# Prompt attention in one block against two chunks with a middle state, and sample keys and values stacked by matmul against by transfer

## What is computed

```python
D = bcum[..., :, None] - bcum[..., None, :] + li[..., None, :]      # causal
inter = bcum + m[..., None]
m_t = jnp.maximum(inter, jnp.max(D, axis=-1))
w_intra, w_inter = jnp.exp(D - m_t[..., None]), jnp.exp(inter - m_t)
s = jnp.einsum('bhjd,bhsd->bhjs', qc, kc) * w_intra
num = einsum('bhjs,bhsd->bhjd', s, vc) + w_inter[..., None] * einsum('bhvk,bhjk->bhjv', C, qc)
C_new = decay[..., None, None] * C + jnp.einsum('bhs,bhsv,bhsk->bhvk', w_s, vc, kc)
```

## Time and profile before

| | |
|---|---|
| median of 3 runs | 941.18 us (940.92 to 941.48) |
| span of the profiled execution | 940.7 us |
| the four heads | about 75 to 430 us of it |
| TensorE busy (matmul / weight load) | 928.3 / 907.8 us |
| VectorE, ScalarE, GpSimd busy | 772.2, 464.4, 106.7 us |

### The profile page before, as it was taken

One profiled execution on the slowest core, in us unless ns is written; L12 is line 12 of the kernel. 1 busy time (PEld: TensorE's weight loads), 2 busy tenths in 40 slices (PEclk: granted clock), 3 DMA queues, 4 the chain that ended last, 5 costly groups with the idle time before them and its releaser, 6 DMA issues. The chain is left out here.

```text
span 940.7 us, 18449 instructions
## 1 busy us (share of the span) xinstructions
PE 928.3 (99%) x6833; PEld 907.8 (96%) x6833; DVE 772.2 (82%) x1231; ACT 464.4 (49%) x684; POOL 106.7 (11%) x110
## 2 busy tenths in 40 slices
PE   8999999999999999999999999999999999999996
PEld 8999999999999999999999999999999999999995
DVE  6899985988698869876455569999888999889997
ACT  6654452445336324634833345456545555455664
POOL 3011330042006001500231000000000000000001
PEclk9999999999999999999999999999999999999998
DMA  6245216211620352042342222233222223232122
GB/s 219 68 150 198 69 57 224 90 45 56 246 90 23 134 191 90 23 150 87 117 140 68 89 73 84 90 108 106 102 90 91 90 68 113 90 116 109 46 91 100
DMA packets 22460, 98.56 MB, mean 105 GB/s; under 512 B 2929, under 2 KB 5122, under 8 KB 17909
## 3 DMA queue, kind: packets, MB, share of 16 engines
q1 hardware_dynamic: 19576, 77.13, 24.9%
q0 software_dynamic: 1984, 19.72, 5.7%
q10 hardware_dynamic: 832, 0.88, 0.3%
HBM read 85.28 MB, written 12.44 MB: 104 GB/s over the span
## 5 line engine op out<-in xcount | busy, mean ns | idle before, releaser
L1301 PE MATMUL ps<-h_hi,w_hi 128*128 128x288 f32 x896 | 193.7, 298 | 0.0
L1301 PE MATMUL ps<-h_lo,w_hi 128*128 128x288 f32 x896 | 191.7, 295 | 0.0
L1301 PE MATMUL ps<-h_hi,w_lo 128*128 128x288 f32 x896 | 191.4, 295 | 0.0
L793 ACT ACTIVATE w_hi<-raw 128x1024 fp32r<-128x1024 f32 x76 | 80.4, 1058 | 177.4 <-PE ps L1301 174.2
L1301 PEld LDWEIGHTS ps<-h_hi,w_hi 128*128 128x128 f32 x896 | 143.5, 189 | 1.3 <-issue 0.6
L1301 PEld LDWEIGHTS ps<-h_hi,w_lo 128*128 128x128 f32 x896 | 144.3, 189 | 0.0
L1301 PEld LDWEIGHTS ps<-h_lo,w_hi 128*128 128x128 f32 x896 | 144.2, 188 | 0.0
L1692 DVE TENSOR_TENSOR w_lo<-raw,w_hi 128x1024 fp32r<-128x1024 f32 x76 | 94.2, 1240 | 48.9 <-ACT w_hi L793 48.8
L1917 DVE SCALAR_TENSOR_TENSOR conv<-a_p,vec,conv x120 | 97.6, 813 | 0.2
L1569 PE MATMUL ps<-cols_b,late 128*128 128x288 f32 x432 | 62.8, 295 | 0.1
L1569 PE MATMUL ps<-cols_a,main 128*128 128x288 f32 x432 | 62.9, 295 | 0.0
(11 more groups left out here) (362 smaller groups left out, 1857.3 us busy)
## 6 DMA issues: line engine op xcount, KB each, us to landing
raw<-w_head_in SPq DMA_DIRECT2D x40, 512.0 KB, 3.5
raw<-w_fp_in SPq DMA_DIRECT2D x18, 1024.0 KB, 4.9
cs<-st_c_in POOLq DMA_DIRECT2D x4, 2048.0 KB, 9.6
c_s_out<-cs POOLq DMA_DIRECT2D x4, 2048.0 KB, 7.7
raw<-w_fo_in SPq DMA_DIRECT2D x8, 1024.0 KB, 4.9
x<-xT_in SPq DMA_DIRECT2D x16, 288.0 KB, 4.1
raw<-w_cgcv_in SPq DMA_DIRECT2D x8, 512.0 KB, 3.6
raw<-w_ga_in SPq DMA_DIRECT2D x8, 512.0 KB, 3.5
```

Of the source, the lines that this page charges most:

```text
L793: act.activation(w_hi[:, s, :], raw[:, s, :], ACT.Copy).then_inc(hi_ready, 1)
L1301: last = pe.matmul(ps[:, 2 * s + b, 0:HALF], wt[:, w, k * P:k * P + P], src[:, k, b * HALF:b * HALF + HALF], start=(k == 0 and wt is w_hi ...
```

## The change

The prompt's 512 tokens are taken as two chunks of 256. Scores and PV are computed within a chunk only (S widths 256, 128, 256, 128; six pairs of blocks instead of ten). The state after 256 tokens (`CM`, "middle state") is computed after unit 6 from the first two key blocks, copied by ScalarE to `cm32`, and split into `cm_hi` (ScalarE) and `cm_lo` (VectorE). The queries of the second chunk are weighted (`wq`, `qt`) and split (`qt_hi` by ScalarE, `qt_lo` by VectorE), and twelve fp32r products add their reading of the middle state into the PV banks of blocks 2 and 3. CP takes the last two key blocks only, and VectorE adds the decayed middle state to it, reading the bank (before, ScalarE copied). The placement matmuls, `place3` and ScalarE's `stk` copies go; instead ScalarE issues six transfers per head from SBUF to SBUF, and TensorE and GpSimd wait for them. `wvs` is in two tensors now, and `wvn` lies over k alone, so that it no longer waits for the last use of q. A few rows of the setup (decay exponents) are changed accordingly.

```diff
-READER = ["dve"] * 5 + ["act"] * (5 + 1 + 2 + 5 + 2) + ["dve"] * (8 + 1 + 3)
+READER = ["dve"] * 5 + ["act"] * (5 + 1 + 2 + 5) + ["dve"] * (2 + 8 + 1 + 3)
-W_OFF = [0, 512, 896, 1152, 1280]
+S_END = [TP // 2, TP // 2, TP, TP]
+W_OFF = [0, 256, 384, 640, 768]
...
@@ GpSimd, per head
-                    pool.wait_ge(act_read, h * ACT_USES + (START + READER[:K_USE + g].count("act") + 1))
-                    pool.tensor_tensor(wvs[0:3 * GT, g * SG:g * SG + SG, :],
+                    pool.wait_ge(stk_placed[g], h * 48 + 48)
+                    pool.tensor_tensor(wvs[g][0:3 * GT, :, :],
...
@@ ScalarE, per head
-                    for t in range(s + 1, NB):
+                    for t in range(s + 1, S_END[s] // P):
...
+                for t in range(CHUNK):
+                    at = (CHUNK + t) * P
+                    act.activation(wq[:, t * P:t * P + P], negm[...at:at + P...], ACT.Exp, bias=dec[...D_Q + t...])\
+                        .then_inc(w_ready, 1)
                 hi_of(3)
                 for j in range(4, 6):
                     hi_of(j)
                     evac_bias(h, j, halves(qkv[:, 2, :, :], j - 4))
+
+                act.wait_ge(qt_ready, h + 1)
+                act.activation(qt_hi[:, :, :], qt[:, :, :], ACT.Copy).then_inc(pvhi_ready, 1)
...
                 act.activation(inter[0:TS, :], bank(I_USE)[0:TS, 0:HD + SB], ACT.Copy).then_inc(act_read, 1)
+                act.wait_ge(kvsplit_ready, h * 2 + 2)
                 for g in range(2):
-                    use(K_USE + g)
-                    act.activation(stk[0:3 * GT, g, :], bank(K_USE + g)[0:3 * GT, :], ACT.Copy).then_inc(act_read, 1)
+                    for r, src in enumerate(stacked):
+                        act.dma_start(stk[r * GT:r * GT + GT, g, :].rearrange("p (c v) -> p c v", c=2).bitcast(F32),
+                                      src[g * GT:g * GT + GT, :, :].bitcast(F32)).then_inc(stk_placed[g], 16)
+                for k in range(2):
+                    use(CM_USE + k)
+                    act.activation(cm32[:, k, 0:VE], bank(CM_USE + k)[:, 0:VE], ACT.Copy).then_inc(act_read, 1)
 
                 act.wait_ge(dve_read, h * DVE_USES + (START + 5))
                 act.activation(w2_hi[:, :], wts[:, 0:W_OFF[NB]], ACT.Copy).then_inc(pvhi_ready, 1)
                 act.wait_ge(act_read, h * ACT_USES + (START + 5))
                 act.activation(v_hi[:, :, :], kvn[:, 0:NB, HD:2 * HD + 2], ACT.Copy).then_inc(pvhi_ready, 1)
+                act.wait_ge(act_read, h * ACT_USES + (START + 8))
+                act.activation(cm_hi[:, :, :], cm32[:, :, :], ACT.Copy).then_inc(pvhi_ready, 1)
...
-                act.wait_ge(cp_free, h + START)
-                for k in range(2):
-                    use(CP_USE + k)
-                    act.activation(cp[:, k, :], bank(CP_USE + k)[:, 0:VE], ACT.Copy).then_inc(act_read, 1)
@@ TensorE, per head
-                    t0, n, rows_ = (s * P, TP - s * P, P) if s < NB else (TP, TS, TS)
+                    t0, n, rows_ = (s * P, S_END[s] - s * P, P) if s < NB else (TP, TS, TS)
...
-                pe.wait_ge(kvsplit_ready, h * 2 + 2)
-                for g in range(2):            (the eight placement matmuls)
...
+                pe.wait_ge(wv_ready, h * NB + CHUNK)
+                for k in range(2):
+                    use(CM_USE + k)
+                    for s in range(CHUNK):
+                        last = pe.matmul(bank(CM_USE + k)[:, 0:VE], kvn[:, s, k * P:k * P + P], wvn[:, s, :],
+                                         start=(s == 0), stop=(s == CHUNK - 1))
                     last.then_inc(attn_ready, 1)
                 head_unit(7)
...
-                        pe.wait_ge(pvlo_ready, h * 2 + 2)
+                        pe.wait_ge(pvlo_ready, h * N_PV + 3)
+                    if t == CHUNK:
+                        pe.wait_ge(pvlo_ready, h * N_PV + 4)
-                        for s in range(t + 1):
+                        for s in range(t - t % CHUNK, t + 1):
...
+                        for k in range(2 if t >= CHUNK else 0):
+                            at = (t - CHUNK) * P
+                            for q_, c_ in ((qt_hi, cm_hi), (qt_hi, cm_lo), (qt_lo, cm_hi)):
+                                last = pe.matmul(bank(PV_USE + t)[:, 0:VE + 1], q_[:, k, at:at + P], c_[:, k, :],
+                                                 start=False, stop=(k == 1 and q_ is qt_lo))
...
-                    for s in range(NB):
+                    for s in range(CHUNK, NB):                      (CP)
...
+                for g in range(2):
+                    pe.wait_ge(stk_placed[g], h * 48 + 48)
                 pe.wait_ge(wvs_ready, h * 2 + 2)
@@ VectorE, per head
+                dve.wait_ge(w_ready, h * N_W + N_W)
+                dve.wait_ge(gb_used, h * 2 + START)
+                dve.tensor_tensor(qt[:, :, :], qkv[:, 0, :, CHUNK * P:TP], wq[...], ALU.mult).then_inc(qt_ready, 1)
                 lo_of(4)
                 split_lo(h * PER_HEAD + (U_B + 7), 1)
...
                 taps(5)
+                dve.wait_ge(pvhi_ready, h * N_PV + 1)
+                dve.tensor_tensor(qt_lo[:, :, :], qt[:, :, :], qt_hi[:, :, :].bitcast(F32), ALU.subtract)\
+                    .then_inc(pvlo_ready, 1)
...
-                use(I_USE)
                 for s in range(NB):
-                    dve.wait_ge(act_read, h * ACT_USES + (START + s + 1))
-                    dve.tensor_scalar(wvn[:, s, :], kvn[:, s, HD:2 * HD + 1], hcol(I_WS + s), None, ALU.mult)\
+                    dve.tensor_scalar(wvn[:, s, :], kvn[:, s, HD:2 * HD + 1], hcol(I_WV[s]), None, ALU.mult)\
                         .then_inc(wv_ready, 1)
...
+                dve.wait_ge(pvhi_ready, h * N_PV + 4)
+                dve.tensor_tensor(cm_lo[:, :, :], cm32[:, :, :], cm_hi[:, :, :].bitcast(F32), ALU.subtract)\
+                    .then_inc(pvlo_ready, 1)
 
                 lo_of(6)
                 lo_of(7)
...
                 dve.tensor_tensor(small[:, 1, :], small[:, 1, :], small[:, 0, :], ALU.mult).then_inc(hvar_ready, 1)
+                dve.wait_ge(cp_free, h + START)
+                for k in range(2):
+                    use(CP_USE + k)
+                    dve.scalar_tensor_tensor(cp[:, k, :], cm32[:, k, 0:VE], dec[...D_MID...],
+                                             bank(CP_USE + k)[:, 0:VE], ALU.mult, ALU.add).then_inc(dve_read, 1)
                 for b in range(SB):
                     use(CS_USE + b)
```

More of the change, by code:

```diff
@@ L247, in build @@
         warm = sb("warm", 1)
+        tmp_base = place[0]
         tmp = sb("tmp", [2, T])
@@ L319, in build @@
         cp = sb("cp", [2, VE])
+        cm32 = sb("cm32", [2, VE + 1])
+        cm_lo = sb("cm_lo", [2, VE + 1], F32R)
         cs_lo_base = place[0]
@@ L1796, in _ @@
             first = slice(TP, T, SL)
-            steps.on(dve.tensor_tensor(t8[:, :], lf[:, first], m0[:, :], ALU.add))
+            steps.on(dve.tensor_tensor(t8[:, 0:SB], lf[:, first], m0[:, :], ALU.add))
             steps.on(dve.tensor_tensor_scan(ft[0:NH, :], seg[:, :], lf[:, :], 0.0, ALU.mult, ALU.add))
```

141 lines of the change are left out of this document (79 added, 62 removed).

## The result

The changed kernel takes 959.16 us (median of 4 runs, 957.41 to 959.4) against 941.33 (940.92 to 941.66) for the kernel before: a ratio of 1.018, 95% interval 1.0165 to 1.0194. The profiled execution has a span of 957.8, 17.1 more than the profile of before. The forecast was 948.8 with a range of 939 to 956: the direction was right, and what was forecast (+7.6) is less than half of what came (+17.8).

A forecast was written before the change was run, and what follows sets the result against it. TensorE, busy 99%, was taken as the bound; 2.65 us less matmul work per head would be outweighed by waits, mainly for VectorE at the third state update: 941.2 + 4 x 1.9 = 948.8 us, range 939 to 956.

The forecast's parts named there:

- wait in the scores: Fourth score block: TensorE waits for VectorE to read the first block's bank, +0.7 us per head.
- six issues on ScalarE: ScalarE's queue ahead of the weights' high part: six transfer issues at 0.33 to 0.41 each, 2.0 to 2.5 us.
- split of unit 8: VectorE's list: this split begins at 219.45 instead of 218.17, 1.3 us late, or 220.05 with late landing.
- third update: TensorE's third state update can start at 230.3 against 228.53, after VectorE's read frees the bank.
- D: The forecast case for the whole kernel: 944 to 953 us, 58% chance.
- E: Clock falls in the 3 us wait, three k-steps cost twice: +2 to +3 us per head more, 957 to 960; 9%.
- +1.9 per head: Net delay taken for each of four heads, between first-order and late-landing results, nearer the first; +7.6 us in all.
- the walk's first result: First-order walk through one head to the third state update: +1.75 us per head.
- rival F: Transfers slow or each issue at 0.63 us: +3 us per head, 953 to 955; 4%.
- the ledger of matmul work: TensorE per head: scores -1.70, placement -0.95, weights times values 0, state 0; sum -2.65 us.
- rival B: Port free: GpSimd's products out of VectorE's way, third state update 1.0 us earlier, 937.1 us; 15%.
- 0, but moved forward: State matmuls: four ahead of unit 7, four behind; sum unchanged, 1.70 us per head moved forward.

The follow-up runs named there:

- e1: Changed kernel with twelve matmuls of a constant, into columns nobody reads, filling TensorE's wait ahead of the third state update: 952.24 us.
- e13: e10 with ScalarE reading the end state's two banks again, VectorE adding the middle state in SBUF after the state updates: 937.81 us.
- e10: Changed kernel with SyncE issuing the six transfers and ScalarE making the high parts of weights and values before waiting for the middle state: 946.98 us.
- e3: Changed kernel with one of GpSimd's two products per head left out, the states of samples 4 to 7 not computed: 952.59 us.
- e5: Changed kernel with convolution taps moved from ahead of the middle state and from behind the split of unit 8 to behind the state updates: 956.68 us.
- e6: e5 with VectorE's split of unit 7's weights also put behind the products of scores and decay weights: 956.17 us.
- e12: Changed kernel with the taps and splits of e6 and the SyncE issues and ScalarE order of e10, state updates at their old places: 945.68 us.
- e9: Kernel before, with only its placement matmuls and ScalarE's two copies replaced by the six ScalarE-issued transfers: 956.71 us.
- e7: Kernel before, with only one edit: VectorE, not ScalarE, reads the end state's two banks: 943.73 us.
- e4: Changed kernel with the six transfers per head issued by SyncE's queue instead of ScalarE's: 957.52 us.
- e2: Changed kernel with ScalarE reading the end state's banks again, VectorE adding the middle state in SBUF after the eight updates: 944.22 us.

## Why the prediction was right and where it was wrong

By its own steps, in us after the start of the scores (forecast on 193.04, measured on 198.23):

| step | forecast | measured |
|---|---|---|
| wait in the scores | 0.7 | 0.63 |
| scores, without it | 3.1 | 3.35 |
| wait ahead of the middle state, and its start | 0.9, 17.7 | 0.79, 17.72 |
| six issues on ScalarE | 2.0 to 2.5 | 3.84 |
| landing of a transfer | 1.9 | 2.0 |
| first product of GpSimd | 20.5 | 20.54 |
| high part of the weights | 20.3 | 21.62 |
| split of unit 8 | 26.4 to 27.0 | 26.79 |
| from there to the third update | 10.84 | 11.06 |
| third update | 37.3 | 37.85 |
| wait ahead of it | 2.8 | 2.63 |
| clock behind it | stays | halves |

**The step that failed is the choice between D and E: that the clock stays through the wait.** The prediction had the wait of nearly 3 us, named the fall of the clock behind it, priced it at 2 to 3 us per head and its outcome at 957 to 960, and gave it 9%. It happened in all four heads and the time was 959.2. e1 shows it as cause: with the same wait filled, the kernel takes 952.2 and D's own range of 944 to 953 holds. The price was too high; it is 7.0 in all, not 8 to 12. That E's total of 957 to 960 was met all the same is partly luck: the waits cost more than the +7.6 under it (e1: +10.8), and the two errors cancel. The 9% were too few. The one row on the matter, showed half the clock where TensorE works with gaps, and there was no row of a pause of this length inside full work that left the clock alone: the waits of the kernel before lay at its ends. And the range was said to take in the lower part of E, but it ends at 956 and E begins at 957, so it held nothing of E. The Trainium skill, TensorE: Matmul & The Clock Gate, Part 1, has idle stretches throttle the array; here the trace agrees (0.50 of the clock from 237.4 to 240.8, behind 2.63 us of waiting).

**A term mis-sized: +1.9 per head was +2.4** (37.85 against 35.49). Against the walk's first result, +1.75, that is 0.6 us more: 0.4 come ahead of the split of unit 8 and 0.2 in the list behind it. Issues took 0.64 each and not 0.33 to 0.41; the forecast's upper bound, 0.63, was the truth. So rival F's cost of an issue came true, but not its +3 per head: a high part 1.3 us later delays the split by 0.4, because, by the prediction's own walk, the low part would have stood behind the first product anyway. Also the ledger of matmul work is -2.43 per head and not -2.65: scores -1.44 (4.79 to 3.35; I took a record's whole duration difference, but the next matmul starts before a record ends), placement -1.05, products +0.14, states -0.08. It closes: 88.50 - 2.43 + the 1.40 of waits in e13 is 87.47, and e13's heads are 87.4 to 87.6 apart.

**Right for the wrong reason: the bound of the third update.** I took VectorE's list from the split of unit 8 as the only thing that sets it, and rival B (937.1) as what happens when that list starts early. There are two bounds, and both belong to the change. The list ends 37.85 after the scores. The chain behind the products, from TensorE's last one over ScalarE's copy and the normaliser to the bank, needs 5.78 us (223.99 to 229.77 in e10), and the move of half the end state to an earlier place left 4.07 to hide it. I booked that move as "0, but moved forward"; with half of the end state's 3.39 us gone from there, the time from the end of the products to TensorE's demand fell from 5.64 to 4.07, at the one place that had none to give. Therefore e3, e5, e6, e10 and e12 all keep 1.7 us, and B would have given about 947, not 937: e10 is close to that case, with the list starting 3.9 us earlier than in the changed kernel.

**What of the change costs what.** The transfers alone: +15.1 us (e9). The bank's reader alone: +2.1 (e7). The chunks with the transfers off the path: +5.3 (e10). The same with the bank given back to ScalarE: -4.0 (e13). The whole: +17.8. They don't add, since they hold up the same TensorE and both e9 and the whole pay for the clock. That a saving of 1.05 us of placement cost so much has two reasons, which e4 and e10 separate: 3.84 us of issues in front of the high parts, and the two products of GpSimd moved into VectorE's low parts. By the rule of the Trainium skill, SBUF — State Buffer, Who interferes with whom, a VectorE operation with two inputs in SBUF and a GpSimd operation that reads SBUF want the same pair of ports, and whichever issues first holds it for the whole instruction. The traces agree: the low part of the middle state takes 0.69 us alone (e3) and 2.15 beside GpSimd (e10), the split of unit 8 1.22 and 2.91.

**What stays open.** With what the clock fell: behind the same 1.71 us it stayed at 1.00 in the first three heads of e10 and in all of e12, and fell (0.98 as the mean of the head) in the last one of e10 and in the first three of e3, e5 and e6. These three have other waits of 0.6 to 1.1 us some 8 to 11 us ahead of it, but so do their last heads, where the clock stayed; no run took that apart. Nor is it shown why it stayed down longer in the first head of the changed kernel, of e4 and of e9 than in the others. A kernel of the chunks alone, with placement by matmul kept, was not tried, so the price of the chunks is known only with the transfers beside them.

## What to carry to other kernels

Moving matmuls forward is not free because their sum stays: ask whose chain they covered, and compare the time from the chain's start to TensorE's next demand, before and after. When the forecast has the bound engine standing still for microseconds in a stretch where it never did, price the slower clock behind the pause as the likely case, and read pace and not busy share to see it. Before a small matmul is traded for transfers, count each issue on the issuing engine's queue and look at what stands behind it there; and give a bank's read to the engine that is idle, not to the one whose list is full, since that one edit was worth 15 us here (e2), and 9 with the other delays gone (e10 to e13).

## What was not expected of the hardware

- An issue of a transfer from SBUF to SBUF holds ScalarE's queue for 0.64 us (24 records of 610 to 762 ns) and SyncE's for as long (592 to 741), for 64 KB that land 2.0 us later.
- The clock can fall after the work has begun again: 1.3 us behind the end of the pause in the second head of the changed kernel, 1.0 in that of e9. In the first head of both it fell 0.6 and 1.0 us before the pause ended.
- A pause of 1.7 us was enough in some heads and not in others (e10, e12).
- Twelve matmuls on a constant that fill a wait give back 7 us of 959 (e1), without any wait being shorter.
